# Differential attention written out as 16 steps with one more step of lag, the last key norms in free score banks, and the first output product taken depth by depth

## The reference, cut to what matters

```python
qd = _rmsnorm(df_q.reshape(b, s, DF_HEADS, 2, DF_HEAD_DIM), q_norm_g)
kd = _rmsnorm(df_k.reshape(b, s, DF_HEADS, 2, DF_HEAD_DIM), k_norm_g)
...
s1 = q1 @ k1 * inv + bias;  s2 = q2 @ k2 * inv + bias      # causal, bias = -slope[head] * distance
p1, p2 = softmax(s1), softmax(s2)
df_o = (p1 - lam * p2) @ v
...
df_out = rmsnorm(df_o, subln_g) * (1 - lam_init) * silu(df_g)
out = x + gate * (concat(sb_out, df_out) @ w_out)
```

## Time and profile before

| | |
|---|---|
| median of 3 runs | 1682.78 us (1681.72 to 1683.64) |
| the profiled execution | 1682.47 us |
| its span in the profile | 1680.7 us |
| PE busy in the span | 1602.3 us (95%) |
| DVE busy | 1125.2 us (67%) |
| ACT busy | 717.9 us (43%) |
| stretch that the change touches | about 1538 us to the end |

### The profile page before, as it was taken

One profiled execution on the slowest core, in us unless ns is written; L12 is line 12 of the kernel. 1 busy time (PEld: TensorE's weight loads), 2 busy tenths in 40 slices (PEclk: granted clock), 3 DMA queues, 4 the chain that ended last, 5 costly groups with the idle time before them and its releaser, 6 DMA issues.

```text
span 1680.7 us, 23383 instructions
## 1 busy us (share of the span) xinstructions
PE 1602.3 (95%) x8495; PEld 1339.7 (80%) x8495; DVE 1125.2 (67%) x1723; ACT 717.9 (43%) x1329; POOL 245.2 (15%) x214
## 2 busy tenths in 40 slices
PE   4899999999999999899998999999999999999788
PEld 3687888888888979898997898888888987766566
DVE  6699788899897723467766575656635616886664
ACT  3333451313224543366665542322224525776441
POOL 0122013233220000123222011111100010000110
PEclk9899999999999999899999999999999999999999
DMA  9565257576763133300000344344422321111101
GB/s 336 193 228 177 84 201 258 186 269 250 233 225 106 56 125 126 106 2 2 0 0 1 101 176 156 138 143 136 136 86 95 104 94 57 51 50 50 50 0 50
DMA packets 106736, 203.24 MB, mean 121 GB/s; under 512 B 6025, under 2 KB 11414, under 8 KB 106646
## 3 DMA queue, kind: packets, MB, share of 16 engines
q1 hardware_dynamic: 106646, 202.01, 35.3%
HBM read 199.90 MB, written 2.10 MB: 120 GB/s over the span
## 4 chain that ended last, share of the span: by engine, by line
PE 75%; DVE 13%; ACT 3%; issue 3%; DMA 3%; POOL 1%; SPq 1%; DVEq 0%; ACTq 0%; POOLq 0%
PE PS L1998 41%; PE PS L1957 15%; PE PS L2324 4%; DVE MACC L1225 4%; DVE WL L1191 3%; PE PS L2305 2%; PE PS L2288 2%; PE PS L2287 1%; ACT WH L703 1%; PE PS L2319 1%; POOL MROW L479 1%; PE PS L2240 1%; PE PS L2453 1%; PE PS L2370 1%; PE PS L2412 1%
## 5 line engine op out<-in xcount | busy, mean ns | idle before, releaser
L703 ACT ACTIVATE WH<-RAW 128x2048 fp32r<-128x2048 f32 (+1 forms) x112 | 210.0, 1886 | 362.9 <-DMA RAW<-in_ff_w_in_dram 220.2
L1191 DVE TENSOR_TENSOR WL<-RAW,WH 128x2048 fp32r<-128x2048 f32 (+1 forms) x107 | 276.3, 2602 | 132.4 <-ACT WH L703 132.4
L479 POOL PARTITION_ALL_REDUCE MROW<-MACC x30 | 142.2, 4741 | 597.6 <-DVE MACC L1225 597.6
L1998 PE MATMUL PS<-WH,HIDh 128*128 128x512 f32 (+1 forms) x576 | 219.9, 382 | 4.6 <-DVE HIDl L1509 3.8
L1998 PE MATMUL PS<-WL,HIDh 128*128 128x512 f32 (+1 forms) x576 | 219.3, 381 | 0.0
L1998 PE MATMUL PS<-WH,HIDl 128*128 128x512 f32 (+1 forms) x576 | 219.3, 381 | 0.0
L1998 PE MATMUL PS<-HTh,WH 128*128 128x512 f32 (+1 forms) x520 | 202.6, 390 | 0.4 <-DVE WL L1191 0.4
L1998 PE MATMUL PS<-HTl,WH 128*128 128x512 f32 (+1 forms) x520 | 202.5, 389 | 0.0
L1998 PE MATMUL PS<-HTh,WL 128*128 128x512 f32 (+1 forms) x520 | 202.4, 389 | 0.0
L1225 DVE SCALAR_TENSOR_TENSOR MACC<-MRAW,CS,MACC 128x512 f32<-128x512 f32 x182 | 136.8, 752 | 9.2 <-DMA MRAW<-in_ada_w_dram 1.0
L1998 PEld LDWEIGHTS PS<-WH,HIDh 128*128 128x128 f32 x576 | 109.7, 190 | 25.7 <-issue 5.0
(11 more groups left out here) (320 smaller groups left out, 3187.9 us busy)
## 6 DMA issues: line engine op xcount, KB each, us to landing
MRAW<-in_ada_w_dram SPq DMA_DIRECT2D x46, 1024.0 KB, 7.4
RAW<-in_ff_w_in_dram SPq DMA_DIRECT2D x32, 1024.0 KB, 5.5
RAW<-in_ff_w_out_dram SPq DMA_DIRECT2D x32, 1024.0 KB, 5.1
RAW<-in_w_in_dram SPq DMA_DIRECT2D x16, 1024.0 KB, 5.3
MRAW<-in_w_ada_dram SPq DMA_DIRECT2D x12, 1024.0 KB, 8.7
RAW<-in_a_w_in_dram SPq DMA_DIRECT2D x8, 1024.0 KB, 9.9
MRAW<-in_kv_ada_w_dram SPq DMA_DIRECT2D x8, 1024.0 KB, 6.1
RAW<-in_kv_w_dram SPq DMA_DIRECT2D x6, 1024.0 KB, 5.2
```

What stands on the lines that cost most here:

```text
L479: pool.partition_all_reduce(MROW[:], MACC[:], P, RADD).then_inc(m_red, 1)
L703: act.activation(WH[:, wslot(u), 0:width(u)], RAW[:, u % 4, 0:width(u)], ACT.Copy).then_inc(w_hi, 1)
L1191: dve.tensor_tensor(WL[:, u % 4, 0:width(u)], RAW[:, u % 4, 0:width(u)], WH[:, wslot(u), 0:width(u)].bitcast(F32), ALU.subtract).then_inc( ...
L1998: mm = pe.matmul(po, a, b_, start=(k == 0 and i == 0), stop=(k == KT - 1 and i == len(ops) - 1), skip_group_check=len(ops) > 3)
```

## The change

- The differential stage is 16 written-out steps n = 0 to 15 (n = 4*head + tile) with no register loop on any engine. PE makes the scores of step n+2, then the transposes of step n-1 (before: of the step n itself) and the values of step n-2 (before: n-1). ACT makes the exponentials of n+2 and then the copy of n-1. DVE makes the difference of n, the maxima of n+2 and the output of n-3. `DB` has six buffers for it in place of four, and the reciprocals four column pairs in place of two.
- The four units that nothing reads are gone, as are POOL's fourth restaging and the copy of the slope column.
- `lo(109)` stands behind the 16 steps on DVE.
- The norms 6 and 7 are both done in stick-breaking head 6, in banks 0 and 1, whose scores have been read by then; the product behind them waits only for bank 7's own eviction. Head 7 has no norm.
- The first scores wait for all 8 norms (before: 5).
- The first output product takes depths 4 to 7 as depths 0 to 3: each depth with all four row tiles.

```diff
+    def norm_bank(i):
+        return 7 if i < 6 else i - 6
...
-            norm_root(h)
+            for i in ((h,), (6, 7), ())[max(h - 5, 0)]:
+                norm_root(i)
...
+        for n_ in range(DF_STEPS + 1):                       # ACT
+            if n_ + 2 < DF_STEPS:
+                df_exps(n_ + 2)
+            if n_ >= 1:
+                df_copy(n_ - 1)
...
+        negmaxes(0)                                          # DVE
+        negmaxes(1)
+        for n_ in range(DF_STEPS + 3):
+            if n_ < DF_STEPS:
+                difference(n_)
+            if n_ + 2 < DF_STEPS:
+                negmaxes(n_ + 2)
+            if n_ >= 3:
+                scaled_out(n_ - 3)
+
         lo(2 * n.chunk + 1)
-        with dve.Fori(0, DF_HEADS) as h:
...
-            pe.wait_ge(dn_sq, h + 1)                         # PE, stick-breaking head h
-            pe.wait_ge(ev_a, units + 2 * h + 1)
-            pe.matmul(PS[:, 7, :], BONE[:], DSQ[h][:], start=True, stop=True).then_inc(dn_ss, 1)
+            if h < 6:
+                pe.wait_ge(ev_a, units + 2 * h + 1)
+            for i in ((h,), (6, 7), ())[max(h - 5, 0)]:
+                pe.wait_ge(dn_sq, i + 1)
+                pe.matmul(PS[:, norm_bank(i), :], BONE[:], DSQ[i][:], start=True, stop=True).then_inc(dn_ss, 1)
             if h < SB_HEADS - 2:
                 make_z(h + 2)
-            pe.wait_ge(dn_sd, h + 1)
+            if h < 6:
+                pe.wait_ge(dn_sd, h + 1)
+            else:
+                pe.wait_ge(ev_a, units + 2 * h + 1)
             product(kind, 2 * (h % 2) + 1, 7)
...
+        for n_ in range(DF_STEPS + 2):                       # PE
+            if n_ + 2 < DF_STEPS:
+                df_scores(n_ + 2)
+            if 1 <= n_ <= DF_STEPS:
+                df_turn(n_ - 1)
+            if n_ >= 2:
+                df_values(n_ - 2)
...
+            elif by_depth:
+                order = [(k, b) for k in range(KT) for b in range(4)]
...
-        chunk("B", HTh, HTl, early=(SBH, SBL), between=turn_outputs)
+        chunk("B", HTh, HTl, early=(SBH, SBL), between=turn_outputs, by_depth=True)
```

More of the change, by code:

```diff
@@ L218, in program @@
     FQ = at("FQ", [P, 2, T], F32, o_macc + 4096)
-    DB = at("DB", [P, 4, 512], F32, o_ht)
-    DT = at("DT", [P, 2, 512], F32, o_htl)
+    DB = [at(f"DB{i}", [P, 512], F32, o_ht + 2048 * i if i < 4 else o_htl + 2048 * (i - 4)) for i in range(6)]
+    DT = at("DT", [P, 2, 512], F32, o_htl + 4096)
     DO = at("DO", [P, 4, 512], F32, o_hid + 16384)
@@ L606, in pool_program, with stage_df @@
             pool.tensor_copy(ZK[s, e, :], SKT[s, j, :]).then_inc(z_sk, 1)
-        def stage_df(half, head, done):
+        def stage_df(half, head):
             staged = (d_sa, d_sb)[half]
@@ L627, in pool_program @@
         pool.wait_ge(dn_n, 1)
-        stage_df(0, 0, 0)
-        stage_df(1, 0, 0)
+        stage_df(0, 0)
+        stage_df(1, 0)
         pool.wait_ge(dn_n, 4)
-        with pool.Fori(0, DF_HEADS) as h:
+        for h in range(1, DF_HEADS):
             for half in range(2):
-                pool.wait_ge(d_sc, h * 8 + (4 + 4 * half))
-                pool.sem_inc(pool_passed, 1)
-                stage_df(half, (h + 1) % DF_HEADS, h + 1)
+                pool.wait_ge(d_sc, 8 * h - 4 + 4 * half)
+                stage_df(half, h)
     BLOCKS = 8
@@ L1134, in act_program, with df_exps, df_copy @@
         act.wait_ge(z_pv, SB_HEADS)
[L1136 to L1155, removed]
+        def df_exps(n_):
+            for u in (2 * n_, 2 * n_ + 1):
+                d = u % 6
+                L = P * (n_ % TT + 1)
+                act.wait_ge(d_nm, u + 1)
+                if n_ >= 3:
+                    act.wait_ge(d_t, n_ - 2)
+                act.activation(DB[d][:, 0:L], PS[:, u % 4, 0:L], ACT.Exp, bias=SM[:, u % 4:u % 4 + 1],
+                               accum_out=SM[:, 4 + u % 4:5 + u % 4]).then_inc(d_ex, 1)
+        def df_copy(n_):
+            L = P * (n_ % TT + 1)
+            act.wait_ge(d_t, n_ + 1)
+            if n_ >= 2:
+                act.wait_ge(d_pv, n_ - 1)
+            act.activation(DT[:, n_ % 2, 0:L], PS[:, 4 + n_ % 2, 0:L], ACT.Copy).then_inc(d_pt, 1)
+        df_exps(0)
+        df_exps(1)
+        for n_ in range(DF_STEPS + 1):
[3 more added lines that the diff above has]
+                df_copy(n_ - 1)
+        act.wait_ge(d_o, DF_STEPS)
         for h in range(DF_HEADS):
-            act.activation(DB[:, h, :], DO[:, h, :], ACT.Square).then_inc(d_sq, 1)
+            act.activation(DB[h][:], DO[:, h, :], ACT.Square).then_inc(d_sq, 1)
         act.wait_ge(d_ss, 4)
@@ new lines, in negmaxes, with difference @@
+        def negmaxes(n_):
+            for u in (2 * n_, 2 * n_ + 1):
+                dve.wait_ge(d_sc, u + 1)
+                dve.tensor_reduce(SM[:, u % 4:u % 4 + 1], PS[:, u % 4, 0:P * (n_ % TT + 1)], AX_X, ALU.max,
+                                  negate=True).then_inc(d_nm, 1)
+        def difference(n_):
+            L, a, r = P * (n_ % TT + 1), 4 + 2 * (n_ % 2), 8 + 2 * (n_ % 4)
+            first, other = DB[2 * (n_ % 3)], DB[2 * (n_ % 3) + 1]
+            dve.wait_ge(d_ex, 2 * n_ + 2)
+            if n_ >= 4:
+                dve.wait_ge(d_o, n_ - 3)
+            dve.reciprocal(SM[:, r:r + 2], SM[:, a:a + 2]).then_inc(d_rc, 1)
+            dve.wait_ge(d_rc, 2 * n_ + 1)
+            dve.scalar_tensor_tensor(out=SM[:, 30 + n_ % 2:31 + n_ % 2], in0=SM[:, a:a + 1], scalar=SM[:, 41:42],
+                                     in1=SM[:, r + 1:r + 2], op0=ALU.mult, op1=ALU.mult).then_inc(d_rc, 1)
+            dve.wait_ge(d_rc, 2 * n_ + 2)
+            dve.scalar_tensor_tensor(out=first[:, 0:L], in0=other[:, 0:L], scalar=SM[:, 30 + n_ % 2:31 + n_ % 2],
+                                     in1=first[:, 0:L], op0=ALU.mult, op1=ALU.add).then_inc(d_nr, 1)
@@ L2438, in pe_program, with df_scores @@
                 make_z(h + 2)
-            pe.wait_ge(dn_sd, h + 1)
+            if h < 6:
+                pe.wait_ge(dn_sd, h + 1)
+            else:
+                pe.wait_ge(ev_a, units + 2 * h + 1)
             product(kind, 2 * (h % 2) + 1, 7)
-        def scores(u, head, at_, ex=None):
-            i = u % 8 // 2
+        def df_scores(n_):
+            h, i = n_ // TT, n_ % TT
             L = P * (i + 1)
[L2447 to L2461, removed]
+            pe.wait_ge((d_sa, d_sb)[i // 2], 3 * h + 3)
+            if n_ >= 2:
+                pe.wait_ge(d_ex, 2 * n_ - 2)
+            for e in range(2):
+                out_ = PS[:, (2 * n_ + e) % 4, 0:L]
+                pe.matmul(out_, FQ[:, e, P * i:P * i + P], DK[:, h, 0:L], start=True, stop=False,
+                          skip_group_check=True)
+                pe.matmul(out_, SID[:, i // 2, :], MB[:, 384 - P * i:512], start=False, stop=True,
+                          skip_group_check=True).then_inc(d_sc, 1)
@@ new lines, in df_turn, with df_values @@
+        def df_turn(n_):
+            pe.wait_ge(d_nr, n_ + 1)
+            if n_ >= 2:
+                pe.wait_ge(d_pt, n_ - 1)
+            for kt in range(n_ % TT + 1):
+                mm = pe.transpose(PS[:, 4 + n_ % 2, P * kt:P * kt + P], DB[2 * (n_ % 3)][:, P * kt:P * kt + P],
+                                  IDENT[:])
+            mm.then_inc(d_t, 1)
+        def df_values(n_):
+            h, i = n_ // TT, n_ % TT
+            pe.wait_ge(d_pt, n_ + 1)
+            if n_ >= 2:
+                pe.wait_ge(d_o, n_ - 1)
+            for kt in range(i + 1):
+                mm = pe.matmul(PS[:, 6 + n_ % 2, 0:P], DT[:, n_ % 2, P * kt:P * kt + P],
+                               DV[:, kt, P * h:P * h + P], start=(kt == 0), stop=(kt == i),
+                               skip_group_check=True)
+            mm.then_inc(d_pv, 1)
@@ L2462, in pe_program @@
         pe.wait_ge(dn_n, 8)
+        df_scores(0)
+        df_scores(1)
         pe.wait_ge(ev_a, freed(67)[0])
         pe.wait_ge(z_f, SB_HEADS)
[L2465 to L2487, removed]
-                mm.then_inc(d_t, 1)
-                if i >= 1:
-                    df_values(i - 1)
-            df_values(3)
```

65 lines of the change are left out of this document (18 added, 47 removed).

## The result

The changed kernel takes 1655.14 us (median of 4 runs, 1654.56 to 1655.80) against 1682.25 before; the ratio is 0.9839 with a 95% interval of 0.9822 to 0.9856. The profiled execution took 1654.92 us, its span 1652.9. The size of one term was wrong; which one is seen when the two traces are cut at the same six events.

A forecast was written before the change was run, and what follows sets the result against it. PE's queue plus the places where PE stands still was taken to bound the kernel. Savings of 4.7 + 4.8 + 8.1 + 5.7 = 23.3 us gave 1659.5 us, range 1655.5 to 1667.

The forecast's parts named there:

- Part 1: Norms 6 and 7 in stick-breaking head 6: the products behind start sooner, 4.7 us saved, bounds 2.8 and 4.7.
- Part 2: Last product to first exponential: norm work and a table load go, exponentials start at T+8.2, 4.8 us saved.
- Part 3: The 16 differential steps: PE's waits for DVE's difference go, period 10.2 us, 8.1 us saved, bounds 5.2 and 9.9.
- `lo(109)`: DVE's 2.28 us split, moved behind the steps: hidden by 48 output matmuls; with the unread units it cancels the filling cost.
- Part 4: Output product taken depth by depth: 144 matmuls run without a stop, 5.7 us saved, 4.1 if the clock falls.
- The clock: Rival: granted clock still falls in head 6, at the first steps and in the output product; 1665 us, 18%.
- the stuck lag: Rival: in the 16 steps DVE's order only passes the wait on, period stays near 11.8 us; 1665.8 us, 14%.
- The third: Rival: loop registers cost more than seen; PE's gaps ahead of large scores go, 0.6 us per head; 1657 us, 15%.
- Slower code in sequence: Rival: fetching the written-out code holds each of the 16 steps by over 1.46 us; above 1683 us, 3%.
- The back-edge: Jump from the differential loop's end to its start: no cost seen, so writing out alone gains no stall per head.

The follow-up runs named there:

- e5: Kernel before with only the norm change (norms 6 and 7 both in head 6, banks 0 and 1): 1672.0 us, ratio 0.9938.
- e1: Kernel before with its differential stage written out instead of looped, same order, lag and drain: 1680.74 us, ratio 0.9992.
- e2: Changed kernel with the old lag (transposes of step n, values of n-1), still written out: 1659.06 us, ratio 0.9862.
- e3: Changed kernel with steps 4 to 11 as a register loop of two passes on PE, ACT and DVE, eight `DB` buffers: 1654.89 us, ratio 0.9833.
- e6: Changed kernel with the split of the output weights' second half back between first maxima and first difference on DVE: 1655.26 us, ratio 0.9833.
- e4: Kernel before with only the output product in its new depth-by-depth order: 1676.74 us, ratio 0.9961.
- e9: Changed kernel itself run once more, for what two runs of one kernel differ by: 1654.16 us, ratio 0.9833.

## Why the prediction was wrong

- **Part 1, right.** 4.85 us against 4.7. The clock did not fall behind the norms; two norm pairs took 1.92 us in the chain, not 2.14. The late `lower_hi(7)` cost nothing seen.
- **Part 2, right.** T+8.06 against T+8.2; the table load went, and `hi(109)` was late next, as said. e5 shows both parts without the steps.
- **Part 3, the failed term.** "I take 10.2": the period is 9.18 us. The step that failed is "PE alone would need 10.0 us". It took the 11.78 us less the two flagged waits for PE's own work, although the four turns that the prediction lists itself (2.8, 3.3, 1.1 and 1.9 us) add up to 9.1, and back to back the matmuls take 8.87. The 10.0 held 0.44 us of the same two waits that no flag shows, 0.34 of the drain, and 0.34 of the loop's form. All of it went, and 0.30 us behind ACT's copy came in, so the period is 9.18 and not 8.87. The other 0.2 us of the 10.2 was an allowance for PE and DVE being out of step; that short wait for ACT is all that the trace shows of such. The stage is four periods and a rest: 4 x 10.2 + 2.2 us were forecast, 4 x 9.18 + 2.5 measured. So the periods account for 4.1 us, more than the whole miss of 3.8, and the rest came out 0.3 us longer, although the clock fall, for which 0.5 us stood in it, did not come. That filling and `lo(109)` with the unread units cancel was thus about 0.8 us too favourable.
- **The mechanism of part 3, right.** The two waits for the difference go with the lag and only with it: they stay in e1, are 1.42 us in e2 and absent in the changed kernel and in e3. Of the 2.60 us per head, 0.37 goes with the form, 0.68 with the drain and what else e2 changes (0.28 at the drain itself, 0.40 in shorter waits for the difference), and 1.55 with the lag (e1, e2 and the changed kernel in a row). The lag takes 1.86 us of stands away and brings the 0.30 behind ACT's copy.
- **`lo(109)`, right on the cover, too high on the gain.** Hidden behind the first 48 output matmuls with 3.4 us to spare. I let it cancel the filling cost of one more step; e6 measures it at 0.5 us.
- **Part 4, right.** 5.66 us against 5.7, clock 1.00, and the same in e4 alone. Its 4.1 us of waits was taken start to start: nine matmuls in 6.06 us, where the three flagged waits add up to 3.20. Part 3 had only to be read the same way.
- **The rivals.** The clock and the stuck lag did not happen. The third, that the loop costs more than seen, is right in its direction: "0.6 us per head" was put on it, 0.37 measured in e1 and 0.2 to 0.6 in e3. Its mechanism did not happen: the gaps of 0.24 us of PE's weight loads, marked "issue", stand ahead of the 512-key scores in the changed kernel as before, and what the form cost lay at the back-edge and on DVE. It named 1657 and had 15%. Slower code in sequence did not happen either: of the 9.18 us of a head, 8.87 are matmuls back to back.
- **The back-edge.** "The trace shows no cost of the loop's back-edge" was a misreading: it shows 0.13 us on PE, and 0.39 us on DVE, which made the next head's first difference late. In e3, where PE has no other wait there, the scores behind the back-edge come 0.45 us late, ahead of them 0.29 us of idle PE that no semaphore ended. The Trainium skill, Runtime: NRT & Kernel Launch, section Instruction fetch mechanics, expects a stall at a taken branch whose target is not in the fetched window; the runs agree that a cost exists, but not whether it is a fetch. In the kernel before, the last values of a head (0.9 us of matmuls that had just waited for a copy) stood ahead of it. That they hid most of it is argued, not shown.
- **The range.** Its lower end took "some of the third rival" off the sum of the best bounds; the best bound of part 3, 9.9 us, was itself 2 us short, since it left 10.0 us as PE's floor. The other 0.6 us lies ahead of all that was changed, and that stretch varies by 1.2 us between the two profiles of the changed kernel (1537.61 and 1536.38 in e9), and by over 3 us among all of them. Without it the time would be at the range's lower end: that it lies just outside is chance, that part 3 was 3.8 us off is not.

## What to carry to other kernels

An engine's own need per period is not the period less its flagged waits: add up its instructions from start to start, by shape, where they run back to back (here 8.87 us, where the flags left 9.99). The same sum shows what a stand costs in full (1.31 us for one flagged as 1.09) and finds waits that a busy share of 100% hides. When two engines exchange work in strict order, one more step of lag is worth the waits that it covers, less the short ones that take their place (1.86 against 0.30 us per head here), and it works as well in a loop. A product whose later operands arrive one by one should be ordered by operand, so that each arrival has a full set of matmuls beside the next; that also kept the clock up here.

## What the runs showed of the hardware

Register loops on PE, ACT, DVE and POOL, with their marker increments, cost 0.37 us per head of 54 float32 matmuls when PE waited elsewhere as well (e1 against before), and a back-edge cost PE 0.45 us when it had no other wait there (e3). The granted clock stayed at 1.00 behind stands of 1.51 and 0.90 us at the start of the steps (changed kernel), and behind two of 1.58 and 1.56 us, 2.5 us apart, at their end (e2). It had fallen behind one of 1.92 us in head 6, and in the output product before with the fourth of four stands of 1.0 to 1.1 us, 2 us apart; in e1 and e5, with the same order there, it fell with the third and stayed down longer (0.76 over the 14 us from depth 4 on, against 0.88). With one such stand alone (e4, changed kernel) it stayed at 1.00. The changed kernel and e9 differ by 1.2 us at norm 6, and by at most 0.05 us in any stretch behind it.
